# First gather of a layer in four pieces between its gates, weight slots handed back in three pieces, router scaled on GpSimd, unread products on TensorE

## What is computed

```python
h = h + mix
xf = rms_norm(h, ffn_norm_g[layer])                     # h * rsqrt(mean(h*h) + eps) * gain
group_probs = softmax(xf @ w_group)                     # 4 logits a token, best one taken
e_logits = (xf @ w_expert_router)[chosen group]         # 8 of 32, two best taken
gate = g_prob * e_prob / sum(e_prob)
y[token] += gate * ((silu(x @ w_gate[e]) * (x @ w_up[e])) @ w_down[e])    # for its two experts
h = h + y
```

## Time and profile before

| | |
|---|---|
| median of 3 runs | 1178.95 us (1177.15 to 1181.53) |
| the profiled execution | 1182.45 us, its span 1180.6 us |
| PE busy | 827.1 us (70%), 5226 passes |
| mean granted TensorE clock | 0.855 |
| DMA | 438 MB, mean 371 GB/s over the span |
| chain that ended last | DMA 47%, PE 40%, issue 7% |
| PE waits for pick before the first gather, layer 0 and 1 | 0.77 and 0.78 us |

### The profile page before, as it was taken

The page is one execution under the profiler, slowest core; times in us unless marked ns, Lnnn a source line. Parts: engine busy times, 40 slices in busy tenths (PEclk is TensorE's granted clock), DMA queues, the critical chain, the costliest instruction groups (busy, mean ns, idle before and its releaser), DMA issues.

```text
span 1180.6 us, 12530 instructions
## 1 busy us (share of the span) xinstructions
PE 827.1 (70%) x5226; PEld 419.0 (35%) x5226; DVE 156.6 (13%) x417; ACT 155.2 (13%) x340; POOL 66.5 (6%) x84
## 2 busy tenths in 40 slices
PE   7999989483738383838689898764656564656595
PEld 6555675140304030303244576322222222221233
DVE  1142431000000000000023534000000000000003
ACT  2245131000000000000020444000000000000002
POOL 0010020000000000000001452000000000000000
PEclk9999999797969687968799998978787877787898
DMA  9942656999999999999999445999999999999992
GB/s 382 422 154 86 277 221 266 430 428 428 428 427 426 428 428 429 428 429 429 427 428 407 157 178 220 410 429 426 429 426 429 428 427 427 428 430 428 427 427 105
DMA packets 34556, 438.00 MB, mean 371 GB/s; under 512 B 3920, under 2 KB 3920, under 8 KB 8528
## 3 DMA queue, kind: packets, MB, share of 16 engines
q1 hardware_dynamic: 33936, 434.92, 88.0%
q10 hardware_dynamic: 576, 2.44, 0.5%
HBM read 436.30 MB, written 1.05 MB: 370 GB/s over the span
## 4 chain that ended last, share of the span: by engine, by line
DMA 47%; PE 40%; issue 7%; DVE 2%; SPq 2%; POOL 1%; ACT 1%; POOLq 0%; DVEq 0%; ACTq 0%
PE bank L1076 17%; DMA arena<-in_w_gate 9%; DMA ring<-in_w_down 9%; PE bank L834 9%; DMA arena<-in_w_up 8%; DMA arena<-in_w_down 7%; DMA ring<-in_w_up 7%; DMA ring<-in_w_gate 7%; PE bank L972 4%; PE bank L862 3%; SPq L403 2%; PE bank L1051 1%; PE bank L813 1%; PE bank L1112 1%; PE bank L1133 1%
## 5 line engine op out<-in xcount | busy, mean ns | idle before, releaser
L1076 PE MATMUL bank<-ring,hg 128*32 128x512 f32 x1792 | 292.5, 711 | 274.5 <-DMA arena<-in_w_gate 80.2
L1076 PEld LDWEIGHTS bank<-ring,hg 128*32 128x32 f32 x1792 | 78.0, 128 | 466.1 <-issue 374.7
L1076 PE MATMUL bank<-arena,hg 128*32 128x512 f32 x256 | 140.9, 713 | 0.0
L1076 PE MATMUL bank<-ring,arena 128*32 128x512 f32 x704 | 108.5, 648 | 34.6 <-DMA ring<-in_w_down 18.1
L834 PE MATMUL bank<-ring,hg 128*128 128x512 f32 x256 | 112.9, 595 | 0.0
L1548 DVE TENSOR_TENSOR arena<-arena,bank 128x512 f32<-128x512 f32 x16 | 11.0, 688 | 562.1 <-PE bank L1076 562.1
L1051 PEld LDWEIGHTS bank<-arena,hr 128*128 128x128 f32 x512 | 63.6, 206 | 13.5 <-issue 11.7
L1051 PE MATMUL bank<-arena,hr 128*128 128x128 f32 x512 | 66.6, 293 | 1.6 <-DVE arena L1517 1.6
L834 PEld LDWEIGHTS bank<-ring,hg 128*128 128x128 f32 x256 | 47.7, 190 | 55.8 <-issue 54.7
L972 PE MATMUL bank<-arena,ring 128*128 128x256 f32 x256 | 65.0, 392 | 1.4 <-ACT arena L782 1.4
L1076 PEld LDWEIGHTS bank<-ring,arena 128*32 128x32 f32 x704 | 31.8, 118 | 93.9 <-issue 80.3
(11 more groups left out here) (178 smaller groups left out, 568.7 us busy)
## 6 DMA issues: line engine op xcount, KB each, us to landing
ring<-in_w_up SPq DMA_DIRECT2D x56, 2048.0 KB, 21.7
ring<-in_w_gate SPq DMA_DIRECT2D x50, 2048.0 KB, 19.9
ring<-in_w_down SPq DMA_DIRECT2D x48, 2048.0 KB, 19.7
arena<-in_w_down SPq DMA_DIRECT2D x14, 2048.0 KB, 27.9
arena<-in_w_up SPq DMA_DIRECT2D x8, 2048.0 KB, 29.7
arena<-in_w_gate SPq DMA_DIRECT2D x8, 2048.0 KB, 27.7
ring<-w_ab SPq DMA_DIRECT2D x6, 2048.0 KB, 30.6
ring<-in_w_gate SPq DMA_DIRECT2D x6, 1536.0 KB, 15.0
```

Of the source, the lines that this page charges most:

```text
L1076: op = pe.matmul(dst[rows, :], lhsT[:, q, rows], unit[s][:, q, cols], start=(q == 0), stop=(q == steps - 1))
```

## The change

It has four parts. (1) Before its first projection PE makes 12 products of `ones` with `ones` into bank 7; nothing reads them. (2) GpSimd multiplies the router by the norm's gain, one operation a layer, at the start; the logits are then made from `hT`, so they wait for `h_done` and not for `scaled`; `turn_rows` waits for `scaled` instead. (3) PE makes three products of 256 columns behind the last turned rows and two behind the ranks, into bank 7, which nothing reads. (4) The first gather of a layer is made in four pieces of two chunks, each into a bank of its own; VectorE evacuates pieces 0 and 2, ScalarE 1 and 3, and PE makes two of the eight steps of the gates behind each. The slots are handed back, and loaded anew, in three parts: a quarter behind piece 0, a quarter behind piece 1, a half behind the last. The transposition for `rounds` comes behind these gates, and the counts of `gathered`, `xe` and `xe_high` are shifted accordingly.

```diff
-LOW = 2 * DE
+PIECES = [slice(0, 2 * DE), slice(2 * DE, 4 * DE), slice(4 * DE, UNIT)]
...
+        def first_bank(l, pair):
+            return (4, 5, 7, OUT_BANKS[l][0])[pair]
...
 SP, experts(l)
-                sp.wait_ge(m["low_used"], 1)
-                for k, (e, j) in enumerate(opening):
-                    sp.dma_start(home(LOOP_SLOTS[l][k])[:, 0:LOW], expert_flat(l, e, j // QUAD)[:, 0:LOW]).then_inc(m["low_landed"], 16)
-                sp.wait_ge(m["used"], 1)
-                for k, (e, j) in enumerate(opening):
-                    sp.dma_start(home(LOOP_SLOTS[l][k])[:, LOW:UNIT],
-                                 expert_flat(l, e, j // QUAD)[:, LOW:UNIT]).then_inc(m["landed"][k], 16)
+                for part, cols in enumerate(PIECES):
+                    if part < 2:
+                        sp.wait_ge(m["low_used"], part + 1)
+                    else:
+                        sp.wait_ge(m["used"], 1)
+                    for k, (e, j) in enumerate(opening):
+                        sp.dma_start(home(LOOP_SLOTS[l][k])[:, cols], expert_flat(l, e, j // QUAD)[:, cols]).then_inc(
+                            m["low_landed"] if part < 2 else m["landed"][k], 16)
...
 GpSimd
             inverse_rms(0)
+            pool.wait_ge(gains_in, 16)
+            pool.wait_ge(late_in, 16)
+            for l in range(DEPTH):
+                op = pool.tensor_tensor(router[:, l], router[:, l], spread(gains[:, 2 * l + 1, :], ROUTER), ALU.mult)
+            op.then_inc(router_scaled, 1)
...
 ScalarE
+                def take_first(pair):
+                    act.wait_ge(m["gathered"], pair + 1)
+                    act.activation(flat(xeT[:, 2 * pair:2 * pair + 2, :]), bank[first_bank(l, pair)][:, 0:S],
+                                   ACT.Copy).then_inc(m["xe_high"], 1)
...
-                take_high(0)
+                take_first(1)
+                take_first(3)
                 silu(0, first=True)
...
 TensorE
+            def stay_busy(n, lhsT, rhs):
+                for _ in range(n):
+                    pe.matmul(bank[7][:, 0:rhs.shape[1]], lhsT, rhs, start=True, stop=True)
+
+            pe.wait_ge(ones_set, 1)
+            stay_busy(12, ones[:], ones[:])
...
             def logits_of(l, k):
-                pe.wait_ge(scaled, KD * (2 * l + 1) + k + 1)
+                pe.wait_ge(h_done, KD * 2 * l + k + 1)
                 if k == 0:
-                    pe.wait_ge(late_in, 16)
+                    pe.wait_ge(router_scaled, 1)
                 for b in range(NB):
                     lo = b * LOGIT_PITCH
-                    op = pe.matmul(bank[FREE_BANKS[l][0]][:, lo:lo + ROUTER], hg[:, k, b * P:(b + 1) * P],
+                    op = pe.matmul(bank[FREE_BANKS[l][0]][:, lo:lo + ROUTER], hT[:, k, b * P:(b + 1) * P],
...
             def turn_rows(l, high):
+                pe.wait_ge(scaled, KD * (2 * l + 1) + 4 * high + 4)
...
                 turn_rows(l, 1)
+                stay_busy(3, ident, hg[:, 0, :])
...
                           skip_group_check=True).then_inc(once["ranked"], 1)
+                stay_busy(2, ident, hg[:, 0, :])
...
+                def gather_first(pair):
+                    if pair == 0:
+                        pe.wait_ge(m["pick"], 1)
+                        pe.wait_ge(hr_done, l + 1)
+                    for k in range(2):
+                        for b in range(NB):
+                            op = pe.matmul(of_block(bank[first_bank(l, pair)], k), hr[:, b, 2 * pair + k, :], pick[:, b, :],
+                                           start=(b == 0), stop=(b == NB - 1))
+                    op.then_inc(m["gathered"], 1)
+
+                def first_gates():
+                    gather_first(0)
+                    for pair in range(4):
+                        if pair < 3:
+                            gather_first(pair + 1)
+                        pe.wait_ge(m["xe_high" if pair % 2 else "xe"], pair // 2 + 1)
+                        op = four(0, 0, bank[6], xeT, KD, slice(0, DE), part=(2 * pair, 2 * pair + 2))
+                        if pair < 2:
+                            op.then_inc(m["low_used"], 1)
+                    op.then_inc(m["used"], 1)
...
-                        pe.wait_ge(m["low_landed"], 16 * QUAD)
-                    for q in range(steps):
-                        if place == 0 and kind == 0 and q == LOW // DE:
-                            op.then_inc(m["low_used"], 1)
+                        pe.wait_ge(m["low_landed"], 2 * 16 * QUAD)
+                    for q in range(*(part or (steps,))):
...
+                    if first:
+                        first_gates()
+                        pe.wait_ge(once["fullest"], l + 1)
+                        pe.transpose(bank[FREE_BANKS[l][0]][0:1, FULLEST:FULLEST + P], fullest, ident).then_inc(once["fullest_row"], 1)
+                    else:
+                        pe.wait_ge(m["xe"], i + 2)
+                        pe.wait_ge(m["xe_high"], i + 2)
...
-                gather(0)
-                pe.wait_ge(once["fullest"], l + 1)
-                pe.transpose(bank[FREE_BANKS[l][0]][0:1, FULLEST:FULLEST + P], fullest, ident).then_inc(once["fullest_row"], 1)
                 quad(0, 0, first=True)
...
 VectorE: take_first(pair) as on ScalarE, signalling xe; take_first(0) stands behind the ranks of
 the later passes and ahead of the gates' values, take_first(2) where take_low(0) stood.
```

More of the change, by code:

```diff
@@ L268, in hybrid_trunk @@
         over_rms_done = sem("over_rms_done")
+        router_scaled = sem("router_scaled")
         hr_turned = sem("hr_turned")
@@ L715, in copy_weights @@
                     act.activation(pick_wT, bank[7][:, 0:S], ACT.Copy).then_inc(m["pickT_sb"], 1)
+                def take_first(pair):
+                    act.wait_ge(m["gathered"], pair + 1)
+                    act.activation(flat(xeT[:, 2 * pair:2 * pair + 2, :]), bank[first_bank(l, pair)][:, 0:S],
+                                   ACT.Copy).then_inc(m["xe_high"], 1)
                 def take_high(i):
-                    act.wait_ge(m["gathered"], 2 * i + 2)
+                    act.wait_ge(m["gathered"], 2 * i + 4)
                     act.activation(flat(xeT[:, 4:8, :]), bank[5][:], ACT.Copy).then_inc(m["xe_high"], 1)
-                take_high(0)
+                take_first(1)
+                take_first(3)
                 silu(0, first=True)
@@ L1042, in experts @@
                           skip_group_check=True).then_inc(once["ranked"], 1)
+                stay_busy(2, ident, hg[:, 0, :])
                 def gather(i):
                     pe.wait_ge(m["pick"], i + 1)
-                    if isinstance(i, int) and i == 0:
-                        pe.wait_ge(hr_done, l + 1)
                     for high in range(2):
@@ L1053, in gather, with four @@
                         op.then_inc(m["gathered"], 1)
-                def four(place, kind, dst, lhsT, steps, cols, strips=range(QUAD)):
+                def gather_first(pair):
[17 more added lines that the diff above has]
+                    op.then_inc(m["used"], 1)
+                def four(place, kind, dst, lhsT, steps, cols, strips=range(QUAD), part=None):
                     unit = {}
@@ L1140, in quad @@
                         turn_weights(i)
-                    pe.wait_ge(m["xe"], i + 1)
-                    pe.wait_ge(m["xe_high"], i + 1)
-                    if not first:
+                    if first:
[5 more added lines that the diff above has]
+                        pe.wait_ge(m["xe_high"], i + 2)
                         pe.wait_ge(m["hT"], i)
-                    four(place, 0, bank[6], xeT, KD, slice(0, DE)).then_inc(m["used"], 1)
-                    if not first:
+                        four(place, 0, bank[6], xeT, KD, slice(0, DE)).then_inc(m["used"], 1)
                         pe.wait_ge(m["pickT_sb"], i)
@@ L1172, in quad @@
                         return
-                    pe.wait_ge(m["xe"], i + 2)
-                    pe.wait_ge(m["xe_high"], i + 2)
+                    pe.wait_ge(m["xe"], i + 3)
+                    pe.wait_ge(m["xe_high"], i + 3)
                     four(place, 2, bank[4], e_hT, MH, slice(0, HALF)).then_inc(m["down_low"], 1)
                     four(place, 2, bank[5], e_hT, MH, slice(HALF, D)).then_inc(m["used"], 1)
-                gather(0)
-                pe.wait_ge(once["fullest"], l + 1)
-                pe.transpose(bank[FREE_BANKS[l][0]][0:1, FULLEST:FULLEST + P], fullest, ident).then_inc(once["fullest_row"], 1)
                 quad(0, 0, first=True)
@@ L1525, in experts, with take_first @@
                 link(op)
+                def take_first(pair):
+                    dve.wait_ge(m["gathered"], pair + 1)
+                    dve.tensor_copy(flat(xeT[:, 2 * pair:2 * pair + 2, :]), bank[first_bank(l, pair)][:, 0:S]).then_inc(m["xe"], 1)
+                take_first(0)
                 dve.wait_ge(once["group_exp"], l + 1)
@@ L1541, in take_low @@
                 def take_low(i):
```

(4 more changed lines are left out.)

## The result

The changed kernel takes 1165.19 us (1164.0 to 1165.71, 4 runs) against 1178.31 (1177.15 to 1181.53) in the same runs: ratio 0.9883, 95% interval 0.9861 to 0.9904, that is 13.1 us less (11.3 to 16.4). Its profiled execution took 1165.19 with a span of 1163.4, 17.2 us under the span of before.

The account below looks back on a forecast made before the run. PE bounds mixers and routing; afterwards the weight queue's restart and lost streaming set the end. Start 2.3, layer 0 5.8 and layer 1 7.7 sum to 15.8 us: off the median 1178.95, 1163, bounds 1161 to 1166 (1159.5 to 1171 with rivals).

Parts of the forecast that it names:

- rival (b): Whole kernel: only the start products give nothing; 13.5 us gained, 1165.4 us; chance 0.11.
- The start: PE's first projection: twelve products before it raise the clock earlier; 2.3 us gained, bounds 0 and 2.6.
- the tight cover: First weights: third piece of unit 0 lands at 13.5, wanted at 13.7; unit 1 lands at 19.5, wanted at 21.
- Gather's start: First gather of each layer: starts 0.26 us earlier in layer 0 and 2.3 us earlier in layer 1.
- `hr` is next in line: Layer 0's gather: its other input, ready at 175.68, is next to set the start, by only 0.2 us.
- The clock: Last logits to gather: no PE idle time over 0.3 us, clock stays at 1.00, gather at 0.119 us a pass.
- The order: First gather and gates of a layer: 3.9 us from gather's start to first hand-back, against 9.40 before.
- The queue: Weight stream's restart after each routing: earlier hand-back gains 5.8 us in layer 0 and 7.7 us in layer 1.
- but for some 0.5: Layer 1's queue: the 6.75 us lost go except some 0.5, first bytes coming 1.2 to 1.5 us behind the issue.
- Rival (a): Routing: the clock falls all the same, first hand-back 6.6 us after gather's start; 1169, or 1171.5 without start; chance 0.19.
- (c): Second quad's slots not yet free, so the queue's lead is given back; at worst 4 us stay, 1175; chance 0.06.
- (d): Long weight streams: new phase of loads and PE reads lowers their rate; at 418 GB/s 1186 us; chance 0.04.

## Why the prediction was right, and where it was not

The forecast was 15.8 us and 1163; 13.1 and 1165.2 were measured, inside the forecast's own bounds of 1161 to 1166. The total alone would not tell it from rival (b), which had 1165.4 for a start that gives nothing; the pass lengths and the run without the start products do. The mechanism is shown in its four parts; the sizes by its steps:

- **The start**, forecast 2.3: 2.44 in this pair of traces, 2.0 over all of them; the 2.95 of the medians holds a dip of the retention stage as well. Right, and the tight cover (third piece, unit 1) held: 14.06 us for 64 passes. The 12 products ended at 6.64 and not at 6.1 (0.229 us a pass, not 0.209), just as the input was there. The working also took 14.0 us for 64 fast passes and 0.213 for one, which is 13.6: by 7.01/32 the slow passes of before were 11, not 13.
- **Gather's start**, forecast 0.26 and 2.3: 0.36 and 2.18. Right. That `hr` is next in line is not tested.
- **The clock**, forecast "at 1.00": right in the routings of every trace that has the products and the logits from `hT`. Without either it fell. But one argument for it was wrong: that the tail of layer 1 keeps its clock with PE busy 0.76. One trace said so the earlier trace rows; the second trace of the same kernel and that of the logits from `hg` say no. So part 2 of the change, priced as a wait, is also part of what keeps the clock; together it is worth some 3.4 us, by a comparison across groups that its trace bears out.
- **The order**, forecast 3.9 us from gather to hand-back: 3.97. Right.
- **The queue**. In layer 0 all of it arrived. In layer 1 the term "but for some 0.5" was too small: the 8 us from 719 at 314 GB/s lose 8 x (1 - 314/428) = 2.1 us. The first bytes are slow though the queue has only just run empty (152 and 213 GB/s in the two microseconds from 719), and then the opening pieces move at 330 to 390 GB/s for a while. Against that the kernel before was slow behind its own restart for longer than the forecast's window (369 GB/s over 740 to 746, an estimate of 0.8 us). The layer gave 6.9 us, not 7.7. SP's opening issues, forecast at about 177.5 and 720.3, stand at 175.97 and 718.13: earlier by the retention stage's 1.4 us and, in layer 1, by the 0.65 that layer 0 gained behind its restart. I had taken 404 GB/s from a window in which later, larger pieces stood as well. The Trainium skill ("DMA: Bandwidth & Descriptors", Measured (HBM→SBUF, 128 partitions, SWDGE, issued from GpSimd)), which wants 1 MiB or more in a transfer for 75% of the peak, I had dismissed. The traces lie nearer to it than I did, with 380 and 314 GB/s behind the hand-backs of halves of a megabyte, and in layer 0 257 and 277 with quarters against 315 with halves. But all these windows hold the slow first bytes as well, and layer 1 has it the other way, 366 and 370 against 328; so what the size alone costs is not shown.
- **Off the median**. The spans differ by 17.2, the medians by 13.1, since the profiled execution of before was 4 us above its median and that of the changed kernel was not. I took 15.8 off the median as if every execution of before paid what the profiled one paid. Its runs spread over 11 us, those of the changed kernel over 4: what a half clock costs in one trace is one draw. What makes the 4 us is not shown. The dip of the retention stage (1.4 us, not in the forecast) is not likely to be it, since both traces of before have it. An argument only: were the 6.8 us at half clock in each gather 3.4, as without the routing products, each layer of before would be 1.7 us shorter. Nor is it certain that the forecast was too high: the interval of the result, 11.3 to 16.4 us, holds 15.8, and two medians of the kernel before lay 2.1 us apart.

Rival (a) did not come, but its price was off as well: it took the long half clock of before (6.8 us) for the rule, and without the routing products it was 3.4. (b), (c) and (d) are out: the start pays, the lead of layer 0's restart (9.61 us) is there at its end (10.26), and the streams read 428 GB/s after as before. Single parts taken out cost 2.95, 3.5, 6.0 and 3.4 us, in sum 15.8; put together they bring 13.1, so they are near to additive, within the spread of the medians of before. That the sum equals the forecast is chance: the 3.4 is a comparison across groups, and each of the four holds what the clock did in its own runs.

## What to carry to other kernels

Where a long stream follows a stage that waits on the engines, price an edit by when the stream restarts and by how many bytes were missing, and look for the first hand-back: one two steps into the work was worth more here than the full clock in the stage (6.0 us against 3.5). Smaller pieces behind an earlier hand-back gave little here: 1.8 us earlier, 0.3 to 1.0 us gained in layer 0. And a place where the clock falls is a random term: take it from two traces before subtracting it from a median, and count steadier times as a gain of its own.

## What was not expected of the hardware

- The granted clock fell in gaps that did not make it fall in the next execution of the same kernel: in the changed kernel in the retention stage in one of three traces, in the mixer of layer 1 in another. Of the nine traces with the start products and nothing added in the retention stage four show the dip there, of the four without them all four. Whether the start products shift those odds is open.
- Time at half clock once it had fallen: 6.8 us in the first gather of layer 0 in both traces of before, in that of layer 1 in the first of them, and in layer 1's routing with the logits from `hg`; 3.4 us in the gathers without the routing products or with the new order alone, and in every dip of the retention stage. Layer 1's routing in the second trace of before has 3.4 us twice, with the full clock between.
- In the first 14 us the profile's granted clock reads 1.00, while passes of the kernel before take nearly twice as long as later (4 in a microsecond at 9 us, 7 in the changed kernel).
- SP took 1.38 to 1.8 us to issue three transfers in most places, of a quarter, a half or one megabyte alike, but 2.10 in one place for three of a quarter and 2.20 to 2.48 in three places for larger ones. No run shows why.
